# The sample's expert rows take places between the last value rows

## What is computed

```
# peer_ffn, for each token t: xb = rmsnorm(h)
q = xb @ w_peer_q                       # 8 heads, two half keys each
s = q . sub_keys                        # 128 scores per half
best_s, expert = top 16 of the sums of the two top 16s, per head
gate = softmax(best_s)
act  = gelu(sum_d peer_u[expert, d] * xb[d])      # input rows u
y    = h + sum_k gate_k * act_k * peer_v[expert_k, :]   # value rows v
```

## Time and profile before

| | us |
|---|---|
| median of 3 runs | 2474.25 |
| lowest and highest | 2473.24, 2474.29 |
| the profiled execution's own time | 2477.94 |
| its span on the core | 2476.2 |

### The profile page before, as it was taken

How to read it: one execution, slowest core, us unless ns; L and a number is a source line. 1 busy time by engine, 2 the same in 40 slices (tenths; PEclk the granted TensorE clock), 3 DMA queues, 4 the chain that set the end, 5 groups by cost and what they waited for, 6 DMA issues and landing times.

```text
span 2476.2 us, 31871 instructions
## 1 busy us (share of the span) xinstructions
PE 1731.3 (70%) x11105; PEld 705.8 (29%) x11105; DVE 1174.0 (47%) x2800; ACT 349.9 (14%) x744; POOL 1202.0 (49%) x1076
## 2 busy tenths in 40 slices
PE   6787797868829999885599996043777422327878
PEld 1355455724403333332233332010111100001212
DVE  2335436299957105656930055856500155561452
ACT  1123223102201123222111132000000000000000
POOL 0000000036746556756665588887654475444773
PEclk9887898888959999898799998556999855557997
DMA  5000005158999999999999999899999999999995
GB/s 200 21 9 19 10 1 228 46 204 347 410 393 393 391 401 400 399 395 335 377 401 402 399 391 348 287 360 405 404 405 405 408 405 404 404 392 378 363 376 211
DMA packets 254251, 775.33 MB, mean 313 GB/s; under 512 B 36513, under 2 KB 45370, under 8 KB 250762
## 3 DMA queue, kind: packets, MB, share of 16 engines
q0 software_dynamic: 150784, 547.43, 56.8%
q1 hardware_dynamic: 102138, 221.64, 23.9%
q10 hardware_dynamic: 1168, 4.23, 0.4%
HBM read 766.36 MB, written 6.81 MB: 312 GB/s over the span
## 4 chain that ended last, share of the span: by engine, by line
PE 32%; DMA 29%; DVE 12%; issue 11%; POOL 10%; SPq 4%; ACT 1%; DVEq 0%; POOLq 0%; ACTq 0%
DMA arena<-peer_v,idxT 16%; DMA arena<-peer_u,eidx 12%; POOL arena L475 9%; PE ps L1551 8%; PE ps L1357 7%; PE ps L1613 5%; DVE arena L1172 4%; SPq L437 2%; PE ps L1599 2%; SPq L434 2%; PE ps L1411 1%; PE ps L1426 1%; PE ps L1629 1%; PE ps L1792 1%; PE ps L1473 1%
## 5 line engine op out<-in xcount | busy, mean ns | idle before, releaser
L475 POOL DMA_INDIRECT arena<-peer_u,eidx x512 | 634.3, 1239 | 861.1 <-DVE eidx L1082 510.1
L1172 DVE CUSTOM_DVE_ANT_0 arena<-arena 128x1024 f32<-128x1024 f32 x384 | 467.1, 1225 | 558.1 <-DMA arena<-peer_u,eidx 556.1
L475 POOL DMA_INDIRECT arena<-peer_v,idxT x512 | 513.1, 1002 | 361.2 <-PE ps L1551 272.2
L1551 PE MATMUL ps<-arena 128*32 128x512 f32 x2048 | 553.0, 621 | 112.9 <-DMA arena<-peer_v,idxT 110.7
L1613 PE MATMUL ps<-arena 128*128 128x512 f32 x512 | 301.0, 672 | 31.9 <-DMA arena<-kpe_pool 31.9
L1683 PE MATMUL ps<-arena 128*32 128x512 f32 x512 | 119.3, 876 | 236.9 <-DMA arena<-vn_pool 236.9
L1551 PEld LDWEIGHTS ps<-arena 128*32 128x32 f32 x2048 | 102.4, 110 | 426.5 <-DMA arena<-peer_v,idxT 342.3
L724 ACT ACTIVATE arena<-ps 128x512 f32<-128x512 f32 x256 | 151.9, 596 | 454.1 <-PE ps L1613 453.3
L1357 PE MATMUL ps<-arena 128*128 128x512 f32 (+3 forms) x400 | 175.5, 600 | 6.7 <-DVE arena L948 6.3
L1599 PE MATMUL ps<-arena 128*32 128x128 f32 x2048 | 162.1, 282 | 1.3 <-ACT arena L724 1.3
L1172 DVE CUSTOM_DVE_ANT_0 arena<-arena,ps 128x1024 f32<-128x1024 f32 x128 | 153.6, 1219 | 16.0 <-DMA arena<-peer_u,eidx 12.1
(11 more groups left out here) (302 smaller groups left out, 1785.4 us busy)
## 6 DMA issues: line engine op xcount, KB each, us to landing
arena<-kt_pool SPq DMA_DIRECT2D x256, 320.0 KB
arena<-vn_pool SPq DMA_DIRECT2D x256, 320.0 KB
arena<-w_q SPq DMA_DIRECT2D x16, 1024.0 KB, 19.3
arena<-w_in SPq DMA_DIRECT2D x8, 1236.0 KB, 15.4
arena<-w_o SPq DMA_DIRECT2D x16, 512.0 KB, 10.8
arena<-peer_u,eidx POOLq DMA_INDIRECT x512, 10.3
arena<-peer_v,idxT POOLq DMA_INDIRECT x512, 8.8
arena<-kpe_pool SPq DMA_DIRECT2D x256, 16.0 KB
```

Source lines behind the costliest of these rows:

```text
L475: pool.indirect_dma_start(ring[:, q % RING, :], None, table, bass.IndirectOffsetOnAxis(ap=index, axis=0)).then_inc(g[q % RING], 16)
L1172: V_.tensor_tensor_reduce(rows, rows, x, 1.0, 0.0, ALU.mult, ALU.add, acc[:, k:k + 1]).then_inc(u_used, 1)
L1551: return T_.matmul(ps[32 * j:32 * j + 32, i, :], W32[:, j, c, :], ring[:, q % RING, 512 * i:512 * i + 512], start=(c == 0), stop=(c == 31) ...
```

## The change

The sixteen sample rows no longer stand behind the 512th value row. In GpSimd's order the eight input rows stand behind value row 111 of block 3 and the eight sample value rows behind value row 123. `v_row` gives a value row's number in the new order. What frees each place of the ring changes with it. On TensorE `turn_experts_s` moves from row 116 to row 102, the spreads to rows 103, 104 and 109 to 114, and the sample's value sum (now into banks 2 and 3) ahead of row 124. VectorE takes the dot products, the diagonal and the sample's final add ahead of `add_y(3)`; a new semaphore `ys_done` releases the store of `y_sample`. ScalarE loads the gelu table ahead of its wait, and stores `y_sample` ahead of block 3.

```diff
+SU_AT, SV_AT = 112, 124
...
+        def v_row(b, k):
+
+            return 2 * P * b + P + k + (BD * (k >= SU_AT) + BD * (k >= SV_AT) if b == NB - 1 else 0)
...
                 for k in range(P):
-                    if k >= RING:
+                    if b == NB - 1 and k == SU_AT:
+                        pool.wait_ge(idxT_done, NB + 1)
+                        for i in range(BD):
+                            pool.wait_ge(v_used, P * b + k - RING + i + 1)
+                            gather(peer_u, idxS[:, i:i + 1], SU_ROW + i)
+                    if b == NB - 1 and k == SV_AT:
+                        for i in range(BD):
+                            pool.wait_ge(v_used, P * b + k - RING + i + 1)
+                            gather(peer_v, idxS[:, i:i + 1], SV_ROW + i)
+                    if b == NB - 1 and SU_AT <= k < SU_AT + BD:
+                        pool.wait_ge(s_u, k - SU_AT + 1)
+                    elif b == NB - 1 and k >= SV_AT:
+                        pool.wait_ge(sv_used, k - SV_AT + 1)
+                    elif k >= RING:
                         pool.wait_ge(v_used, P * b + k - RING + 1)
...
             gate_exp(4)
-            store_y(3)
+            act.preload_act_table_set("gelu_and_others")
             act.wait_ge(s_u, BD)
             nc.scalar.activation(acc[:, 0:BD], acc[:, 0:BD], ACT.Gelu).then_inc(gelu_done, 1)
-            act.wait_ge(y_done, NB + 1)
+            act.wait_ge(ys_done, 1)
             act.dma_start(y_sample, hs[0:BD, :]).then_inc(stored, 16)
+            store_y(3)
...
-            add_y(3)
             for k in range(BD):
-                q = 2 * P * NB + k
+                q = SU_ROW + k
...
-            dve.wait_ge(s_v, 1)
+            dve.wait_ge(sv_used, BD)
...
-            last.then_inc(y_done, 1)
+            last.then_inc(ys_done, 1)
+            add_y(3)
...
+            def values_s():
+
+                pe.wait_ge(W_done, NB + 1)
+                w8 = W32[:, 0, 0:2, :].rearrange("p c m -> p (c m)")
+                for k in range(BD):
+                    q = SV_ROW + k
+                    pe.wait_ge(g[q % RING], 16 * (q // RING + 1))
+                    for i in range(2):
+                        last = T_.matmul(ps[0:BD, 2 + i, :], w8[:, 8 * k:8 * k + 8],
+                                         ring[:, q % RING, 512 * i:512 * i + 512], start=(k == 0), stop=(k == BD - 1))
+                    last.then_inc(sv_used, 1)
...
-                        48: turn_queries_s, 54: scores_s, 116: turn_experts_s})
...
+                        48: turn_queries_s, 54: scores_s, 102: turn_experts_s, 103: lambda: spread_s(0),
+                        104: lambda: spread_s(1), 109: lambda: spread_s(2), 110: lambda: spread_s(3),
+                        111: lambda: spread_s(4), 112: lambda: spread_s(5), 113: lambda: spread_s(6),
+                        114: lambda: spread_s(7), SV_AT: values_s})
```

More of the change, by code:

```diff
@@ L325, in build @@
         s_xb = sem("s_xb")
-        s_v = sem("s_v")
+        sv_used = sem("sv_used")
+        ys_done = sem("ys_done")
         selT_done = sem("selT_done")
@@ L511, in _ @@
                         pool.wait_ge(u_used, P * (b + 1) + k - RING + 1)
[L512 to L519, removed]
+                    gather(peer_v, idxT[:, gcol(k):gcol(k) + 1], v_row(b, k))
         @block.scalar
@@ L1322, in _ @@
             V_.tensor_tensor(w8d, acc[:, 0:BD], dsm[:, 56:64], ALU.mult).then_inc(W_done, 1)
-            dve.wait_ge(s_v, 1)
+            dve.wait_ge(sv_used, BD)
             for i in range(2):
-                last = V_.tensor_tensor(hs[0:BD, i * 512:(i + 1) * 512], ps[0:BD, i, :],
+                last = V_.tensor_tensor(hs[0:BD, i * 512:(i + 1) * 512], ps[0:BD, 2 + i, :],
                                         hs[0:BD, i * 512:(i + 1) * 512], ALU.add)
-            last.then_inc(y_done, 1)
+            last.then_inc(ys_done, 1)
+            add_y(3)
         @block.tensor
@@ L1548, in half @@
                 def half(k, i):
-                    q = 2 * P * b + P + k
+                    q = v_row(b, k)
                     c, j = k // 4, k % 4
@@ L1794, in spread_s @@
                 last.then_inc(s_xb, 1)
+            def values_s():
[8 more added lines that the diff above has]
+                    last.then_inc(sv_used, 1)
             v_phase(3, {4: turn_latents, 8: heads_by_token, 16: lambda: turn_s(mxs[0:BD, :], 1), 22: lambda: project_s(0), 26: lambda: project_s(1),
                         32: lambda: turn_s(xs2, 2), 40: lambda: queries_s(0, 4), 42: lambda: queries_s(4, 8),
-                        48: turn_queries_s, 54: scores_s, 116: turn_experts_s})
[L1799 to L1804, removed]
-                q = 2 * P * NB + BD + k
-                pe.wait_ge(g[q % RING], 16 * (q // RING + 1))
-                for i in range(2):
-                    last = T_.matmul(ps[0:BD, i, :], w8[:, 8 * k:8 * k + 8],
-                                     ring[:, q % RING, 512 * i:512 * i + 512], start=(k == 0), stop=(k == BD - 1))
-            last.then_inc(s_v, 1)
+                        48: turn_queries_s, 54: scores_s, 102: turn_experts_s, 103: lambda: spread_s(0),
+                        104: lambda: spread_s(1), 109: lambda: spread_s(2), 110: lambda: spread_s(3),
+                        111: lambda: spread_s(4), 112: lambda: spread_s(5), 113: lambda: spread_s(6),
+                        114: lambda: spread_s(7), SV_AT: values_s})
 _OUTS = [
```

3 lines of the change are left out of this document (added).

## The result

The changed kernel takes **2482.1 us** (median of 8 runs, 2477.69 to 2491.39), the kernel before on the same chip 2474.7 (8 runs, 2473.24 to 2477.84): ratio **1.0028** [1.0015, 1.0041]. It is slower, by about 7 us. The profiled execution took 2481.78, its span 2480.0.

What follows compares the result with a forecast made beforehand. Bound: the value rows' stream at the DMA's pace, then a 47.7 us tail on TensorE, to be hidden. Ring waits, stages and sums chained from row 101's end to 2478.1 on the span, +1.9, so 2476.2 on the median; range 2463 to 2483.

Steps and rivals of the forecast that it cites:

- The likeliest case: The forecast itself: ring waits, stage A at the low clock, stage B partly; 2476.2 us, spanning 2470 to 2479, chance 0.45.
- stage A: Spread 2, row 109, spread 3, row 110, spread 4, row 111 on TensorE at 1.2 GHz: 20.5 us, to 2429.1.
- to spread 2 (wait for u0's dot): From row 101's end near 2393.9 until u0's dot is done at 2408.6, TensorE standing 2.7 us.
- until row 112 has landed: Row 111 frees u7's place, row 112 is issued behind u7: 0.3 + 1.24 + 4.3 = 5.8 us, to 2434.9.
- stage B: Row 112, spread 6, row 113, spread 7: first two at 1.2 GHz, last two at 2.4; 10.2 us, to 2445.1.
- to the value sum: u7's dot 1.3, POOL and row 119's landing 0.3 + 4.3, rows 120 to 123 and sv0 6.4: to 2457.4.
- The chain through the ring: Gathers wait for places freed by TensorE's rows and VectorE's dots; the 47.7 us tail is given back, 20.5 as bandwidth.
- rival two: The stream never stalls, sixteen rows cost bandwidth alone: 2453.4 on the span, 2451.5 on the median; chance 0.05.
- The landing of a gather: A gather that meets an idle DMA lands 4.3 us after its issue; taken for u0, row 112 and row 119.
- The alternation: Spreads and rows by turns on TensorE, four passes each: 1.7 us a piece at 2.4 GHz, 3.4 at 1.2.
- Rival three: Clock stays at 1.2 GHz from the wait for u0 through spread 7, all of stage B: 2479.6 to 2483; chance 0.28.
- Rival one: Clock holds at 2.4 GHz in both stages, 2462.6, or falls but is back by row 110, 2466.0; chance 0.22.

Runs made afterwards that it cites:

- experiment 3: The changed kernel run again unedited, twice: 2609.23 against 2604.27 us for the kernel before, ratio 0.9995; the second a single run of 2486.31 us.
- experiment 5: The changed kernel with four idle 128-row matmuls in each of TensorE's two waits: 2591.49 against 2595.76 us, ratio 0.9997; a second time, one run, 2473.33 us.
- Experiment 1: The kernel before with the eight spreads' operands at 128 rows where they had 8: 2578.18 against 2595.76 us, ratio 0.9898.
- The order by turns: The changed kernel with input rows one by one between value rows, 8-row spreads, two versions: ratios 0.9911 and 0.9952 against the kernel before.
- experiments 5 and 6: The second of these: the changed kernel with input rows one by one between value rows, 2565.44 against 2595.76 us; with an earlier turn, 2585.38 against 2604.27.

## Why the prediction was right in its mechanism and short in its size

The range of 2463 to 2483 holds 2482.1. The likeliest case's own range, 2470 to 2479, does not, and +0.28% [0.15, 0.41] lies more on the side of "slower" than in "within 0.2%". The forecast was 5.9 us short. By steps, counted from row 101's end, the sum against the run of the result and against the second run of experiment 3, which comes near the clock that the forecast took (stage A low; in B row 112 low, where the forecast has spread 6 low too):

| step, us (each rounded) | sum | result's run | exp. 3 |
|---|---|---|---|
| to spread 2 (wait for u0's dot) | 14.7 | 15.9 | 16.0 |
| stage A | 20.5 | 15.0 | 21.8 |
| until row 112 has landed | 5.8 | 6.8 | 6.8 |
| stage B | 10.2 | 9.0 | 9.5 |
| to the value sum | 12.3 | 14.3 | 14.5 |
| value sum, rows 124 to 127 | 16.3 | 15.9 | 15.8 |
| to the end of the span | 4.4 | 4.5 | 4.5 |
| sum | 84.2 | 81.4 | 88.9 |

**The chain through the ring: right.** Every wait named stands where it was named: TensorE ahead of spread 2 (4.6 us; I had said 2 to 4) and ahead of row 112, GpSimd ahead of u5, u6, u7 and of rows 118 and 119, and a DMA share of 0.35 to 0.7 in the stages. The naive rival two was wrong; GpSimd does not keep 1.24 us. The waits of TensorE were sized too short: 2.7 us ahead of spread 2 in the sum, and 2.4 ahead of row 112 (5.8 less spread 5), where 4.57 and 4.78 were measured.

**The landing of a gather: too short.** I took 4.3 us from the earlier trace rows for each. Where GpSimd issues one gather behind another, the later ones take longer: in experiment 3's run row 112, the second of two, landed 5.2 us behind its issue (2435.03, next behind u7's at 2433.79, to 2440.22), and row 123, the fifth of a series that begins with row 119, 6.3 us behind its issue, as in the chain of that run:

```profile
2456.40 6.28 DMA arena<-peer_v,idxT
```

In the chain of the result's run the same row took 6.24. A gather by itself did land as I had taken it: row 119 was issued at 2447.06 there and matched at 2451.47. The earlier trace rows is a median of eight gathers with waits between them. This is the +1.0 ahead of row 112 and 2.0 of the +2.2 ahead of the value sum.

**The alternation: sized to the pass, not to the piece.** A spread and the row behind it together take 3.74 us at full clock (experiment 5, 1.91 from 2410.89 to 2412.80, and 1.83) and 7.27 at half (experiment 3, 2411.66 to 2418.93), where eight passes of 0.43 or 0.85 from the earlier trace rows make 3.4 and 6.8. Over stage A this is +1.3, and some 0.7 ahead of spread 2. Another 0.7 there is row 104: GpSimd was let go 2.4 us behind the start of rows 104 to 108 (2406.39 to 2408.77), where I had 1.7. The trace of before had no such piece.

**The clock in stage A: right as a kind, wrong as one value.** It fell at the wait for u0 in all three runs of the changed kernel, for the reason given. How long it stays differs between runs of the same instructions: 7 us of stage A in the result's run, all 21.8 in both others. Rival three put this into its price (2479.6 to 2483) and the median lies there, but its mechanism, stage B wholly low, is in none of the three timelines: row 112 runs low in all of them, and spread 6 is back. That the median lies inside the range is so in part luck, since the range reaches up to it by a clock that did not occur, while the term that was short, the landing of gathers, had no price in any rival. Rival one, where the clock holds, took waits of several us being filled (experiment 5). Its price of 13.6 us below the sum compares with 12.2 measured against the two runs whose clock is near the sum's.

The Trainium skill (TensorE: Matmul & The Clock Gate, section "Why this matters for your kernels") has the clock kept by continuous work. Experiment 3 disagrees as the trace of before did: 0.50 with 21.79 of 21.79 us busy. Experiment 1 shows what decides in this kernel: the same spreads with 128-row operands run at 1.00 with a gap of 0.75 us among them.

**The base: a step that I did not question.** The sum was made against one execution whose tail, 90.3 us, was 2.3 above the mean of two. Counted against the mean, the same sum of 84.2 gives +4.2 (1.9 and 2.3) where I wrote +1.9, and the forecast would have been 2478.5, still within its class. The remaining 3.6 us are of the size of the mis-sized terms above (+4.7 in all in experiment 3's run), less what an early return of the clock gives back in some runs. This account is no closer than the scatter ahead of row 101 lets it be. One sign of being right came true by luck: the last add of VectorE started at 2475.52, within 2474 to 2478, because the stretch ahead was 4.7 us longer than in the trace of before and the tail 2.8 shorter than the sum.

**What is left open.** On the two scattering chips the medians and the tails do not agree in size (experiment 1: 26 us by the ratio, 6 to 11 by the tail; experiment 3: no loss by the ratio, 6 to 11 by the tail). Experiment 3's interval is wide enough for both; that of experiment 1 begins at 12 us, just above its tail. I have not tested what decides for how long the clock stays low. The order by turns changes the turn's and the value rows' places too, and their shares in its 10.9 us are not apart.

## What to carry to other kernels

Late work that shares a ring of buffers with a stream should be dealt in one by one between the stream's items, not as a block as long as the ring: ask of each gather what frees its place, and how fast that happens while the moved work runs. Give TensorE operands of full height where a small one leaves most rows empty: zeros cost nothing here, and full clock was kept in the spreads (15.4 instead of 22 to 25 us). And when an edit is worth some microseconds, compare two or three executions from a point just ahead of it to the end, since one profile of each kernel had the sign wrong.

## What the runs showed of the hardware that I had not expected

- Spreads of 8-row operands with 128-row work beside them ran at 0.95 to 1.00 (experiments 5 and 6). An alternation of one spread and one row that was entered at 0.50 stayed there for 21.8 us in two runs (experiment 3) and came back after 7 in another (the result's), with the same instructions.
- The clock's fall is not at a fixed place: 2.3 us into the spreads of the kernel before in one run, 5.4 in another, which makes the spreads 3.0 us shorter (25.4 and 22.35).
- The row stream, all 128-row work, is not always at full clock either: in the trace of before the stretch from 2386.36 to 2389.78 reads 0.50, behind waits of 1.61 and 0.81 us for rows. I had read the stream as 1.00.
- Idle matmuls, 3.60 us of work for nothing in each of two waits, shorten the tail by some 10 us (94.2 to 84.4, means of three and of two runs).
- A gather of 512 KB that landed 4.3 us after its issue when it stood alone took 5.2 as the second in a row, 6.2 to 6.3 as the fifth.
